# Interleaved weights in pairs of k tiles, and dense matmuls read and written backwards, in a two-block transformer kernel on one core

## What is computed

```python
def first_block(x, ...):                  # D = 1024, D_FF = 2816
    h = _rms_norm(x, norm_mix[l])
    u = h @ w_in[l]                       # 11 + 30 tiles of 128 output columns
    ...
    o_nsa = _nsa(q, kc, vc, ...)          # sparse attention
    o_rwkv, v_first = _rwkv7(rw, ...)     # a linear recurrence
    y = gates[:, :, 0] * (o_nsa @ proj_nsa[l]) + gates[:, :, 1] * (o_rwkv @ proj_rwkv[l])
    x = x + y @ w_out[l]
    x = x + _conv_ffn(_rms_norm(x, norm_ffn[l]), ffn_up[l], ffn_conv[l], ffn_down[l])
    return x
```

## Time and profile before

| | us |
|---|---|
| median of 3 runs | 2433.51 (2431.32 to 2433.78) |
| the profiled execution, its time | 2431.45 |
| the profiled execution, its span from first to last instruction | 2429.6 |

### The profile page before, as it was taken

How to read it: one execution, slowest core, us unless ns; L and a number is a source line. 1 busy time by engine, 2 the same in 40 slices (tenths; PEclk the granted TensorE clock), 3 DMA queues, 4 the chain that set the end, 5 groups by cost and what they waited for, 6 DMA issues and landing times.

```text
span 2429.6 us, 38821 instructions
## 1 busy us (share of the span) xinstructions
PE 2378.4 (98%) x13906; PEld 1953.2 (80%) x13906; DVE 1065.1 (44%) x1843; ACT 935.4 (38%) x1278; POOL 1034.3 (43%) x754
## 2 busy tenths in 40 slices
PE   8999998899999999999999999999999999999999
PEld 6878777778888888888888877888888888888887
DVE  4456475455555522222222855763333448222212
ACT  3345432243555533444423322224444624444322
POOL 3322230035454555455555633443333355555554
PEclk9999999999999999999999999999999999999999
DMA  5211110023232233222233322221222232222332
GB/s 159 70 44 44 61 62 3 3 92 98 87 96 99 99 104 104 95 95 95 95 106 109 101 70 70 86 80 62 87 78 78 70 104 69 95 95 97 102 104 95
DMA packets 60732, 204.21 MB, mean 84 GB/s; under 512 B 10940, under 2 KB 11708, under 8 KB 60380
## 3 DMA queue, kind: packets, MB, share of 16 engines
q1 hardware_dynamic: 55152, 196.45, 24.7%
q10 hardware_dynamic: 5488, 6.44, 0.9%
HBM read 200.76 MB, written 2.10 MB: 83 GB/s over the span
## 4 chain that ended last, share of the span: by engine, by line
PE 87%; DVE 9%; issue 2%; ACT 1%; POOL 1%; DMA 0%; SPq 0%; DVEq 0%; ACTq 0%
PE psum L403 85%; DVE rope_t L2540 2%; DVE qk_st L2539 2%; POOL x L388 1%; PE psum L650 1%; DVE rope_t L2532 1%; DVE qk_st L2542 1%; PE psum L1090 0%; DVE inv L2157 0%; DVE tmp L2458 0%; ACT dd L1437 0%; DVE a_t L2098 0%; PE psum L772 0%; DVE zm L1799 0%; DVE h_lo L1833 0%
## 5 line engine op out<-in xcount | busy, mean ns | idle before, releaser
L376 POOL TENSOR_TENSOR w_lo<-raw,w_hi 128x512 fp32r<-128x512 f32 x732 | 1006.3, 1396 | 1377.3 <-ACT w_hi L1243 1377.3
L403 PE MATMUL psum<-h_hi,w_hi 128*128 128x512 f32 x2128 | 852.8, 401 | 13.7 <-DVE h_lo L1833 10.6
L403 PE MATMUL psum<-h_lo,w_hi 128*128 128x512 f32 x2128 | 835.4, 393 | 0.0
L1243 ACT ACTIVATE w_hi<-raw 128x1024 fp32r<-128x1024 f32 x366 | 386.1, 1055 | 684.7 <-PE psum L403 669.0
L403 PE MATMUL psum<-h_hi,w_lo 128*128 128x512 f32 x2128 | 535.4, 390 | 0.0
L403 PEld LDWEIGHTS psum<-h_hi,w_hi 128*128 128x128 f32 x2128 | 403.5, 190 | 112.4 <-issue 26.6
L403 PEld LDWEIGHTS psum<-h_lo,w_hi 128*128 128x128 f32 x2128 | 403.5, 190 | 83.6 <-issue 3.2
L403 PEld LDWEIGHTS psum<-h_hi,w_lo 128*128 128x128 f32 x2128 | 399.0, 188 | 83.9 <-issue 0.5
L1799 DVE TENSOR_TENSOR tmp<-psum,rst 128x512 f32<-128x512 f32 x100 | 69.1, 691 | 322.5 <-PE psum L403 322.2
L403 PE MATMUL psum<-hid_hi,w_hi 128*128 128x512 f32 x528 | 205.4, 389 | 0.0
L403 PE MATMUL psum<-hid_lo,w_hi 128*128 128x512 f32 x528 | 205.4, 389 | 0.0
(11 more groups left out here) (427 smaller groups left out, 2605.1 us busy)
## 6 DMA issues: line engine op xcount, KB each, us to landing
raw<-in_w SPq DMA_DIRECT2D x366, 512.0 KB, 3.3
x<-in_x SPq DMA_DIRECT2D x4, 512.0 KB, 6.3
x<-in_x ACTq DMA_DIRECT2D x1, 2048.0 KB, 7.9
out_y<-x SPq DMA_DIRECT2D x8, 256.0 KB, 2.3
mask<-in_mask ACTq DMA_DIRECT2D x1, 1536.0 KB
tmp<-in_cmp_w ACTq DMA_DIRECT2D x2, 512.0 KB, 5.7
masks<-in_masks ACTq DMA_DIRECT2D x1, 768.0 KB, 4.3
lora<-in_lora ACTq DMA_DIRECT2D x1, 512.0 KB, 3.2
```

Of the source, the lines that this page charges most:

```text
L376: pool.tensor_tensor(w_lo[:, g.slot, part], raw[:, g.slot, part], w_hi[:, g.slot, part].bitcast(F32), ALU.subtract).then_inc(sem("lo_ready ...
L403: return pe.matmul(out, lhsT, rhs, start=start, stop=stop)
L1243: act.activation(w_hi[:, g.slot], raw[:, g.slot], ACT.Copy).then_inc(sem("hi_ready"), 1)
```

## The change

Two things change, and both touch every dense matmul.

The first is where a weight stands in `w_hi` and `w_lo`. Before, the 128 words of tile k follow each other. After, the tiles 2q and 2q + 1 share 256 words, column by column in turn: word 256 q + 2 c + a is column c of tile 2q + a. ACT and POOL still read `raw` in the old order and write (POOL also reads `w_hi`) in the new one, so their words are two apart. PE loads 128 weights at a step of two words.

The second is the direction of the moving operand. It is read from token 511 to token 0, and the output is written from word 511 to word 0, so each result lands where it did before.

The transfers, the `raw` layout, the waits, the order and the number of instructions on every engine stay the same.

```diff
+        def by_column(t, slot):
+            return t[:, slot].rearrange("p (q c a) -> p q a c", a=2, c=128)
+        def of_raw(slot):
+            return raw[:, slot].rearrange("p (q a c) -> p q a c", a=2, c=128)
+        def weights(t, slot, k):
+            return by_column(t, slot)[:, k // 2, k % 2]
...
             def low_part(g):
                 pool.wait_ge(sem("hi_ready"), g.value(1))
                 for n in range(2):
-                    part = slice(512 * n, 512 * n + 512)
-                    pool.tensor_tensor(w_lo[:, g.slot, part], raw[:, g.slot, part], w_hi[:, g.slot, part].bitcast(F32),
+                    part = slice(2 * n, 2 * n + 2)
+                    pool.tensor_tensor(by_column(w_lo, g.slot)[:, part], of_raw(g.slot)[:, part],
+                                       by_column(w_hi, g.slot)[:, part].bitcast(F32),
                                        ALU.subtract).then_inc(sem("lo_ready"), 1)
...
             def mm_hi(out, slot, k, hi, lo, start):
-                a = w_hi[:, slot, tok(k)]
-                mm(out, a, hi, start, False)
-                mm(out, a, lo, False, False)
+                a = weights(w_hi, slot, k)
+                mm(out[:, ::-1], a, hi[:, ::-1], start, False)
+                mm(out[:, ::-1], a, lo[:, ::-1], False, False)
             def mm_lo(out, slot, k, hi, stop):
-                return mm(out, w_lo[:, slot, tok(k)], hi, False, stop)
+                return mm(out[:, ::-1], weights(w_lo, slot, k), hi[:, ::-1], False, stop)
...
-                act.activation(w_hi[:, g.slot], raw[:, g.slot], ACT.Copy).then_inc(sem("hi_ready"), 1)
+                act.activation(by_column(w_hi, g.slot), of_raw(g.slot), ACT.Copy).then_inc(sem("hi_ready"), 1)
```

## The result

| | us |
|---|---|
| before, median (4 runs) | 2433.65 (2431.32 to 2435.98) |
| after, median (4 runs) | 2493.68 (2491.01 to 2501.02) |
| after / before, 95% interval | 1.0251 (1.0227 to 1.0276) |
| after, the profiled execution: time, span | 2495.47, 2493.7 |

The forecast was 2350 us with a range of 2328 to 2480. The sign was wrong, and the time lies outside the range. In the kernel after, L403 has become L416, L1243 is L1256 and L376 is L388.

A forecast was written before the change was run, and what follows sets the result against it. Taken as bound: start-to-start distance of 8640 dense matmuls, 0.2267 us each. Losing 0.011 each gives 95 us, less 7 and 5 off the path, 83: about 2350 us; own range 2335 to 2392, whole range 2328 to 2480.

The forecast's parts named there:

- The loss of 0.011 us against 0.216: Dense matmuls at full clock: each takes 0.2267 us but would need about 0.216, so about 0.011 is lost.
- (a): PE's weight load at a step of two words; taken together with (b): -0.011 us a matmul, 83 us less.
- (b): PE's moving read and PSUM write backwards; taken together with (a): -0.011 us a matmul, 83 us less.
- lower end: Dense matmul distance: nothing lost any more, 0.216 us, -0.011 a matmul; the upper end was +0.011.
- two readers with equal speed and direction: Weight load and moving read on PE: they keep their distance, meet at the start or never; gains 0.011 us a matmul.
- second rival: PE's weight load: each stretch of memory touched costs the moving read a fixed time; 2516 or 2480 us; chance 0.20.
- The share off the path: Rotations of window attention 7 us, sparse attention and recurrence 5: that much of the 95 us is not gained.
- (c): ACT's rounding writes at a step of two: 1.05 us, factor taken 1.0 (bound 1.54), hidden.
- (d): POOL's split reads `w_hi`, writes `w_lo` at a step of two: 2 x 1.29 us, factor 1.0, hidden.
- No change: Rival for the dense matmuls: loss tied to format or separate load path; 0.2267 stays, 2433 plus or minus 4; chance 0.14.
- slower by POOL: Rival: at a factor over 2.1 POOL's two splits exceed a unit's 5.44 us; 2610 us at 2.3; chance 0.04.
- The projections: Matmuls on `pj_in`, moving tiles 513 words apart: 0.233 us distance before, 0.006 over the common one; predicted to gain too.

The follow-up runs named there:

- e3: Kernel before, but each dense weight load reads one word of each partition 128 times (step 0); 2459.84 us.
- e9: Kernel before, but loads of 96 of the 128 weight columns in all but the first and last matmul of an output tile; 2453.84 us.
- e10: Kernel before, but loads of 64 of the 128 weight columns in all but the first and last matmul of an output tile; 2455.02 us.
- e1: Kernel after without the backwards part: weights at a step of two words, moving operand and output forwards; 2481.30 us.
- e4: Against the step-two-only kernel: four k tiles in turn, a step of four words, everything forwards; 2546.61 us.
- e2: Kernel before with moving operand and output backwards, weights loaded at step one; 2482.61 us.
- e5: Kernel before with only the moving operand read backwards, output written forwards; 2483.19 us.
- e15: Kernel before with all weights moved by 32 bytes, step and direction unchanged; 2478.65 us.
- e12: Kernel after with only ACT's and POOL's stores at step two; PE's loads and directions as before; 2433.81 us.
- e6: Kernel before with only the output written backwards, moving operand read forwards; 2436.10 us.
- e18: Kernel before with all weights moved by 256 bytes; 2435.78 us.
- e14: Kernel before with 64-column loads in all but an output tile's first and last matmul, moving operand and output backwards; 2478.22 us.

## Why the prediction was wrong

**What bounds the kernel: right.** Start-to-start distance of the dense matmuls, 8640 of them; their change alone accounts for the 64 us between the two profiled executions.

**The loss of 0.011 us against 0.216: not shown as something that can be had.** No kernel here had a mean distance under the 227.3 ns of before, neither with loads of half the length, nor with one word, nor from another place; single distances of 224 did occur (e3, e9, e10), paid for by longer ones. The 0.216 came from plain `float32` matmuls and from the lower clock; what `float32r` needs at full clock with no load beside it was never seen. The load's rate, an estimate there (0.107 us for 128 weights), is borne out: from 64 to 128 columns the load grows by (188 - 134) / 64 = 0.84 ns a column, 0.108 us for 128. That equal speeds avoid the loss doesn't follow from it: with the step of two alone (e1) the distance rose. At the lower clock the kernel after is just where the kernel before was, 0.43 us from start to start as in the earlier trace rows (PE's timeline after; the granted clock of 1372 to 1374 us is 0.50):

```profile
1372.47 0.63 PE L416 MATMUL psum<-h_lo,w_hi 128*128 128x512 f32 x1
1372.90 0.63 PE L416 MATMUL psum<-h_hi,w_hi 128*128 128x512 f32 x1
1373.33 0.63 PE L416 MATMUL psum<-h_lo,w_hi 128*128 128x512 f32 x1
```

So the loss belongs to the full clock, as the prediction read it, before and after.

**The value for (a) and (b): this is the step that failed.** Between the bounds of -0.011 and +0.011 I took the lower end; measured was +0.0067 in some stages and +0.010 in others, +0.0074 in the mean. The bounds held it. The choice rested on a picture of two readers with equal speed and direction that meet less often, for which no row spoke. The nearest row was the earlier trace rows: `float32r`, full clock, another access pattern, +0.006. I had it, called it proof that addresses matter, and then took its size for a bound alone and its sign for none. In the rows, a pattern that differs from the common one was only seen to cost. By that row the sum is the 2480 that stands under the second rival, 14 us off; that rival's milder price came near because its size is this row's, and its mechanism, touches, is not what the runs show (e3, e4). In its place they show this: each half of the edit by itself takes the steady 226.7 to 233.3 (e1, e2), the moving read alone does so in the second half (e5), and the place of the weights, with step and direction as before, is worth as much (e15).

**That addresses and meetings matter: right**, and more than I thought: 32 bytes are worth 47 us (2478.65 beside 2431.36). What failed is where the kernel before stands in that. I took its 226.7 for a disturbed state that could be freed, and it is the best mean of all those measured.

**The share off the path: too large, as far as two traces show.** I took 12 of 95 us as lying beside other work. Here 8640 x 7.4 = 64 us came out whole between profiled executions (60 between the medians); in e1 8640 x 6.1 = 53 us of distance gave 2481.06 - 2431.45 = 50. Most of the 12 was to be in the rotations of window attention, where the chain runs on DVE and L403 holds 3.9%. That share hangs on where the window ends: after the last `qk_st` of a head the chain goes over to PE, and a window 5 us later holds more of that (shares by line, 1370 to 1405 us of before; then 1400 to 1435 us of after, which ends about as far behind the rotation):

```profile
by line: DVE rope_t L2540 25.5%; DVE qk_st L2539 24.2%; PE psum L403 16.8%; DVE qk_st L2542 14.5%; issue 11.1%; DVE rope_t L2532 10.4%; DVE qk_st L2578 0.5%; DVE qk_st L1799 0.2%; DVE tmp L1799 0.2%
```

```profile
by line: DVE rope_t L2553 23.4%; DVE qk_st L2552 23.1%; PE psum L416 16.5%; DVE qk_st L2555 14.6%; issue 11.6%; DVE rope_t L2545 10.7%; DVE qk_st L2591 0.5%; DVE qk_st L1812 0.2%; DVE tmp L1812 0.2%
```

The shares are alike, so the chain doesn't tell. The length of a head does. DVE's timeline of before and then of after, at the last `qk_st` of the first head, and the first and the last of the second:

```profile
1398.45 0.68 DVE L2542 TENSOR_TENSOR qk_st<-qk_st,rope_t 32x512 f32<-32x512 f32 x1
...
1448.41 0.68 DVE L2542 TENSOR_TENSOR qk_st<-qk_st,rope_t 32x512 f32<-32x512 f32 x1
...
1475.61 0.68 DVE L2542 TENSOR_TENSOR qk_st<-qk_st,rope_t 32x512 f32<-32x512 f32 x1
```

```profile
1428.69 0.68 DVE L2555 TENSOR_TENSOR qk_st<-qk_st,rope_t 32x512 f32<-32x512 f32 x1
...
1479.60 0.68 DVE L2555 TENSOR_TENSOR qk_st<-qk_st,rope_t 32x512 f32<-32x512 f32 x1
...
1508.01 0.68 DVE L2555 TENSOR_TENSOR qk_st<-qk_st,rope_t 32x512 f32<-32x512 f32 x1
```

A head took 77.2 us and takes 79.3, and in the rotation itself, from the first such `qk_st` of the second head to the last, 27.2 us have become 28.4. So the longer matmuls lengthen the rotation as well, though the chain runs on DVE there. PE waits for `qk_st` no longer than before (1.8 against 1.7 us over the run): the two end at about the same time. Whether a gain would have been lost there no run shows, since none had one.

**(c) and (d), the stores: right.** ACT's factor was 1.12 and POOL's 1.01 (taken: 1.0), and e12 shows them hidden. **No change** and **slower by POOL** didn't happen. **The range** ended at 2480 because I took the dearer part of the second rival, up to 2516, into the fifth that could be left out; the time fell into that part.

**The projections**, predicted to gain, lost too: the earlier trace rows beside the kernel after, (2.06 - 0.39) / 7 = 0.239 us against 0.233 (over all neighbours on `pj_in` 237.7 ns against 233.1):

```profile
566.46 1.11 PE L416 MATMUL psum<-pj_in,w_lo 128*128 128x512 f32 x4
567.41 2.06 PE L416 MATMUL psum<-pj_in,w_hi 128*128 128x512 f32 x8
```

**What stays open.** Why 512 columns take 226.7 ns and not 213 to 216; why a backwards read takes 233.3; why half a load frees nothing; and why both halves together make 0.2333 in some stages and 0.2367 in others (the scatter of the kernel after, 2491 to 2501 us, may be a matter of which stage falls into which; only one of its four executions has a trace). No run has a load from the last column to the first, so my assumption on its direction was neither shown nor refuted. No kernel here beats the kernel before; e6, e12 and e18 equal it.

## What to carry to other kernels

When a matmul stream bounds a kernel, read the start-to-start distance: if it is the same for every matmul and operand, the kernel may stand on a good place of its operands, and any change of address, step or direction has to be priced as leaving it. Take the nearest row with its sign, even if it is only a disturbance in another place, before a mechanism that no row shows. A shift of the weights by a few words is an edit of one line that shows how much the stream depends on the place, and is worth a run before weights are rearranged.

## What the hardware showed beyond that

- Steady distances, the same from one matmul to the next, are few: 226.7 ns (before, e6, e12, e18) and 233.3 (e1, e2, e5, e14), each in most units; in clocks of 1.2 GHz these are 272 and 280, where the lower clock has 512 (427 ns). Other kernels repeat a short pattern, and its mean can be as even: in the third feed-forward part of the kernel after 235 and 238 by turns (mean 236.7), in e15 231, 235, 234, 234 (mean 233.3), in e10 six distances from 224 to 236 (mean 230.0). So a unit of 5.60 us alone doesn't say that the stream is steady; the single starts do.
- Turning the PSUM write around is free (e6: 2436.1 beside 2435.9 us); turning the moving read around costs 47 us (e5: 2483.2).
- A load of 64 columns is recorded with 134 ns, one of 96 with 161 and one of 128 with 188, and a step of four words makes it 310; the mean distances beside them are 230.0, 230.3, 227.3 and 235.2 ns, so none of these lengths sets the matmul's distance by itself.
